# A three-block transformer on one core: the second block's feed-forward network on unnormalised x, its gate product on GpSimd, and the first expert's gather behind its down product

## What is computed

```python
# block 1: 16 experts, each takes the 32 tokens with the largest router weight
gate, idx = lax.top_k(jnp.swapaxes(aff, 1, 2), cap)
xs = jax.vmap(lambda hb, ib: hb[ib])(h, idx)
a, u = einsum(xs, w_gate), einsum(xs, w_up)          # 1024 -> 2048
y = einsum(silu(a) * u, w_down) * gate               # 2048 -> 1024, scattered back and added
...
# block 2
x = x + rmsnorm(merged @ w_out, mix_post_norm)       # norm 6
h = rmsnorm(x, ffn_pre_norm)                         # norm 7
up = causal_dwconv(h @ w_ffn_up, ffn_conv_w, ffn_conv_b)   # 1024 -> 6144, 3 taps along the tokens
f_gate, f_val = jnp.split(up, 2, axis=-1)
f = (gelu(f_gate) * f_val) @ w_ffn_down              # 3072 -> 1024
x = x + rmsnorm(f, ffn_post_norm)                    # norm 8
```

## Time and profile before

| | us |
|---|---|
| median of 3 runs | 1921.76 (1919.69 to 1925.24) |
| the profiled execution | 1920.94 |
| its span, first to last instruction | 1919.2 |
| PE busy in the span | 1516.7 (79%) |
| DVE busy | 717.6 (37%) |
| ACT busy | 597.2 (31%) |
| POOL busy | 36.4 (2%), 40 instructions |

### The profile page before, as it was taken

One profiled execution on the slowest core, in us unless ns is written; L12 is line 12 of the kernel. 1 busy time (PEld: TensorE's weight loads), 2 busy tenths in 40 slices (PEclk: granted clock), 3 DMA queues, 4 the chain that ended last, 5 costly groups with the idle time before them and its releaser, 6 DMA issues.

```text
span 1919.2 us, 25348 instructions
## 1 busy us (share of the span) xinstructions
PE 1516.7 (79%) x10672; PEld 1039.9 (54%) x10672; DVE 717.6 (37%) x1166; ACT 597.2 (31%) x1014; POOL 36.4 (2%) x40
## 2 busy tenths in 40 slices
PE   6999886666665656655666668999999999998897
PEld 4887831111111111111111128999998999898897
DVE  4457600000000000000000006858677886568774
ACT  5434410000000000000000005685666665455653
POOL 0000200000000000000000000000000000000101
PEclk9999897787887887888887779999999999999999
DMA  9556689999999999999999995433363545533330
GB/s 400 220 226 244 264 350 427 429 428 429 428 429 429 429 429 428 429 428 429 429 429 429 428 428 233 182 132 133 140 242 115 193 176 187 189 142 121 137 127 23
DMA packets 48611, 570.30 MB, mean 297 GB/s; under 512 B 4624, under 2 KB 10896, under 8 KB 12048
## 3 DMA queue, kind: packets, MB, share of 16 engines
q1 hardware_dynamic: 43072, 559.96, 71.0%
q10 hardware_dynamic: 5456, 9.15, 1.4%
HBM read 564.89 MB, written 4.19 MB: 297 GB/s over the span
## 4 chain that ended last, share of the span: by engine, by line
PE 50%; DMA 40%; DVE 6%; ACT 3%; issue 1%; POOL 0%; SPq 0%; ACTq 0%; DVEq 0%
PE bank L1521 50%; DMA ring<-in_w_gate 13%; DMA ring<-in_w_up 13%; DMA ring<-in_w_down 12%; ACT work L1922 1%; DMA ring<-in_dense 1%; DVE rstd L2163 1%; ACT weights_high_rounded L1922 1%; DVE ring_rounded L2219 1%; DMA ring<-in_w_ada 1%; ACT L1922 0%; DVE ring_rounded L2230 0%; DVE work L1336 0%; DVE small L1330 0%; DVE small L1316 0%
## 5 line engine op out<-in xcount | busy, mean ns | idle before, releaser
L1521 PE MATMUL bank<-ring,work 128*32 128x512 f32 x3008 | 481.9, 774 | 307.3 <-DMA ring<-in_w_up 126.9
L1521 PEld LDWEIGHTS bank<-ring,work 128*32 128x32 f32 x3008 | 93.2, 126 | 659.3 <-DMA ring<-in_w_up 208.5
L1922 ACT ACTIVATE work<-bank 128x256 f32<-128x256 f32 (+2 forms) x209 | 93.5, 461 | 1089.8 <-PE bank L1521 764.7
L2219 DVE TENSOR_TENSOR ring_rounded<-ring,weights_high_rounded 128x1024 fp32r<-128x1024 f32 x208 | 252.4, 1222 | 118.1 <-ACT weights_high_rounded L1922 117.8
L1922 ACT ACTIVATE weights_high_rounded<-ring 128x1024 fp32r<-128x1024 f32 x244 | 255.3, 1051 | 20.1 <-PE bank L1521 19.7
L2464 DVE TENSOR_TENSOR work<-work,bank 128x512 f32<-128x512 f32 x16 | 16.5, 1033 | 588.8 <-PE bank L1521 588.8
L1521 PE MATMUL bank<-h_high_rounded,weights_high_rounded 128*128 128x256 f32 x1264 | 192.2, 291 | 1.0 <-ACT h_high_rounded L1922 1.0
L1521 PE MATMUL bank<-h_high_rounded,ring_rounded 128*128 128x256 f32 x1264 | 173.1, 278 | 6.3 <-DVE ring_rounded L2219 4.0
L1521 PE MATMUL bank<-h_normed_rounded,weights_high_rounded 128*128 128x256 f32 x1264 | 172.1, 279 | 0.0
L1521 PEld LDWEIGHTS bank<-h_high_rounded,weights_high_rounded 128*128 128x128 f32 x1264 | 165.8, 191 | 11.1 <-issue 10.0
L1521 PEld LDWEIGHTS bank<-h_high_rounded,ring_rounded 128*128 128x128 f32 x1264 | 157.5, 189 | 7.2 <-DVE ring_rounded L2219 4.3
(11 more groups left out here) (248 smaller groups left out, 1265.5 us busy)
## 6 DMA issues: line engine op xcount, KB each, us to landing
ring<-in_w_down SPq DMA_DIRECT2D x64, 2048.0 KB, 16.2
ring<-in_w_gate SPq DMA_DIRECT2D x63, 2048.0 KB, 16.3
ring<-in_w_up SPq DMA_DIRECT2D x61, 2048.0 KB, 16.4
ring<-in_dense SPq DMA_DIRECT2D x60, 2048.0 KB, 7.7
ring<-in_w_ada SPq DMA_DIRECT2D x12, 2048.0 KB, 13.4
work<-in_w_up SPq DMA_DIRECT2D x3, 1024.0 KB, 14.6
bias_diagonals<-work SPq DMA_DIRECT2D x2, 1536.0 KB, 8.8
ring<-in_dense SPq DMA_DIRECT2D x2, 1024.0 KB, 18.5
```

The source lines that it names most:

```text
L1521: return nc.tensor.matmul(o, lhsT, rhs, start=start, stop=stop)
L1922: return nc.scalar.activation(o, i, f, **kw)
L2219: v.tensor_tensor(as_r(w), w, w_high[:, buffer, :], ALU.subtract).then_inc(s.w_low, 1)
```

## The change

- Feed-forward network: PE multiplies x times the norm's gain per channel, not yet divided by the root. `raw_splits` on ACT writes the high halves and squares from X as its tiles come; `add_normed` has a third instruction per tile on DVE, the low half (`split_scaled_low`, already there, an instruction like L2157). PE does the first three units together, tile by tile (`dense_together`); the other units go one by one. The squares of norm 7 are added by POOL, and PE's sum for it stands behind the three units and ahead of the fourth. The matmuls that only kept PE at work are gone there.
- As each unit leaves its bank, DVE multiplies it by the reciprocal root into `SCALED`, four buffers in SBUF (`scaled`). This frees the bank. ACT's tap and DVE's two taps read `SCALED`, a unit later on DVE.
- The gate product and its low half go from DVE to POOL, product k ahead of low half k - 1.
- First expert: `place_slots` goes behind both halves, `gather_rest` behind the down product, and into banks 0 and 1; DVE's copy for expert 1 and ACT's `tokens_in` move accordingly.
- Counts of semaphores in the third block follow.

```diff
@@ -126,7 +126,7 @@
-ADDED_NORMS = (2, 6, 8, 10, 11)
+ADDED_NORMS = (2, 6, 7, 8, 10, 11)
 ADDED_TILES = KT - 2
...
@@ -373,7 +373,7 @@
         UP, FV = tiles3(0, 48), tiles3(48, FT)
-        DO = tiles3(72, 8)
+        DO, SCALED = tiles3(72, 8), tiles3(72, 4)
         LRU_FLAT = tiles(45, 8)
...
@@ -399,6 +399,13 @@
+        def unit_ready(dve, unit):
+            if block_ends(unit):
+                dve.wait_ge(s.ring_used, d2_block(unit) + 1)
+            else:
+                dve.wait_ge(s.dense_mm, units_through(unit))
         def tensor_dense2(pe, dense_unit, unit, act, pu, base=None, first=True, last=True, spare=None):
...
@@ -530,18 +537,13 @@
             awake_through_norm(6, B[6], 4, 4)
-            column_sums(7, spare=B[6])
-            awake_through_norm(7, B[6], 5, 2)
-            for u in range(2 * FT):
-                if u >= 4:
-                    pe.wait_ge(s.conv_step, taps_through(u - 4))
-                unit2(L_UP + u, normed, None if u else "up")
+            dense_together([(d2_block(u), u % UNITS, B[(PU2 + u) % 4], D1_UNITS + u + 1) for u in range(L_UP, L_UP + 3)],
+                           *normed, IN_AT["up"][0])
+            added_sums(7)
+            for u in range(3, 2 * FT):
+                unit2(L_UP + u, normed)
             high, low = by_tile(as_r(UP[:, 0:2 * FT:2, :])), by_tile(as_r(FV))
             for n in range(KT):
-                if n < 4:
-                    pe.wait_ge(s.conv_step, taps_through(2 * FT - 4 + n))
                 for kg in range(3):
...
@@ -696,18 +698,17 @@
             weight_high(D1_UNITS + L_UP - 1 + AHEAD2)
-            squares_of_x(s.x_ready, 2 * KT)
+            raw_splits(2 * KT, HH_plain, par("ffn_pre"))
             root(7)
-            for k in range(KT):
-                split_high(HH[:, k, :], H[:, k, :])
             for u in range(2 * FT):
                 unit_done(d2_block(L_UP + u), block_ends(L_UP + u))
                 if u == 40:
                     act.wait_ge(s.toep_stored, 32)
-                fn(ffn_conved(u), B[(PU2 + L_UP + u) % 4][:, 0:SEQ], ACT.Identity, scale=ffn_weight(u, 2),
-                   bias=par("ffn_conv_b", u, u + 1)).then_inc(s.dense_sb, 1)
+                act.wait_ge(s.dense_sb, PU2 + L_UP + u + 1)
+                fn(ffn_conved(u), SCALED[:, u % 4, :], ACT.Identity, scale=ffn_weight(u, 2),
+                   bias=par("ffn_conv_b", u, u + 1)).then_inc(s.tap_ready, 1)
                 weight_high(D1_UNITS + L_UP + u + AHEAD2)
...
@@ -895,33 +896,37 @@
             dve.wait_ge(s.dense_sb, PU2 + L_UP)
-            add_normed(6, MO2)
+            add_normed(6, MO2, after=lambda k: split_scaled_low(H[:, k, :], X[:, k, :], par("ffn_pre", k, k + 1), HH_plain[:, k, :]))
             weight_low(L_UP - 1 + AHEAD2)
             norm_invert(7)
-            norm_to(7, H, X, par("ffn_pre"), HH)
+            def scaled(u):
+                unit_ready(dve, L_UP + u)
+                v.tensor_tensor(SCALED[:, u % 4, :], B[(PU2 + L_UP + u) % 4][:, 0:SEQ], RS[:, 1, :],
+                                ALU.mult).then_inc(s.dense_sb, 1)
             def tap(u, shift):
                 o = ffn_conved(u)
                 if shift == 1:
-                    dve.wait_ge(s.dense_sb, PU2 + L_UP + u + 1)
+                    dve.wait_ge(s.tap_ready, u + 1)
                 else:
                     dve.wait_ge(s.conv_step, taps_through(u) - 1)
-                v.scalar_tensor_tensor(out=o[:, shift:SEQ], in0=B[(PU2 + L_UP + u) % 4][:, 0:SEQ - shift],
+                v.scalar_tensor_tensor(out=o[:, shift:SEQ], in0=SCALED[:, u % 4, 0:SEQ - shift],
                                        scalar=ffn_weight(u, 2 - shift), in1=o[:, shift:SEQ],
                                        op0=ALU.mult, op1=ALU.add).then_inc(s.conv_step, 1)
-            for k in range(FT):
-                for u in (2 * k, 2 * k + 1):
-                    tap(u, 1)
-                    weight_low(L_UP + u + AHEAD2)
-                    tap(u, 2)
-                    if u % 2 == 0 and k:
-                        split_low(FV[:, k - 1, :], UP[:, 2 * (k - 1), :])
-                dve.wait_ge(s.ffn_gelu, k + 1)
-                dve.wait_ge(s.conv_step, taps_through(2 * k + 1))
-                v.tensor_tensor(FV[:, k, :], FV[:, k, :], UP[:, 2 * k, :], ALU.mult).then_inc(s.act_full, 1)
-            split_low(FV[:, FT - 1, :], UP[:, 2 * (FT - 1), :])
+            for u in range(2 * FT):
+                scaled(u)
+                if u:
+                    tap(u - 1, 1)
+                    weight_low(L_UP + u - 1 + AHEAD2)
+                    tap(u - 1, 2)
+            tap(2 * FT - 1, 1)
+            weight_low(L_DOWN - 1 + AHEAD2)
+            tap(2 * FT - 1, 2)
+            splits_elsewhere(FT)
             weights_low(L_DOWN + AHEAD2, L_EVEN - 1 + AHEAD2)
...
@@ -1009,7 +1014,7 @@
                     if n >= 4:
-                        pe.wait_ge(s.act_full, tile_count("odd_out", n - 4) - KT)
+                        pe.wait_ge(s.act_full, tile_count("odd_out", n - 4) - RAW_SETS * KT)
                     rows = P // len(heads)
...
@@ -1511,7 +1509,22 @@
                 nc.gpsimd.tensor_tensor(as_r(ht), ht, as_r(by_group(HT_HIGH, t, a, b)), ALU.subtract).then_inc(s.ht_low, 1)
-            for i in ADDED_NORMS[1:]:
+            add_squares(6)
+            add_squares(7)
+            def ffn_low(k):
+                pool.wait_ge(s.act_high, tile_count("ffn", k))
+                nc.gpsimd.tensor_tensor(as_r(FV[:, k, :]), FV[:, k, :], as_r(UP[:, 2 * k, :]), ALU.subtract).then_inc(s.act_low, 1)
+            for k in range(FT):
+                pool.wait_ge(s.ffn_gelu, k + 1)
+                pool.wait_ge(s.conv_step, taps_through(2 * k + 1))
+                nc.gpsimd.tensor_tensor(FV[:, k, :], FV[:, k, :], UP[:, 2 * k, :], ALU.mult).then_inc(s.act_full, 1)
+                if k:
+                    ffn_low(k - 1)
+            ffn_low(FT - 1)
+            for i in (8, 10, 11):
                 add_squares(i)
...
@@ -1549,6 +1562,28 @@
                 return ins
+            def dense_together(units, high, low, base):
+                for k in range(KT + 1):
+                    if k < KT:
+                        pe.wait_ge(s.act_high, base + k + 1)
+                        for _, _, bank, counts in units:
+                            if k == 0:
+                                pe.wait_ge(s.w_high, counts)
+                            at = slice(k * P, (k + 1) * P)
+                            mm(bank[:, 0:SEQ], w_high[:, (counts - 1) % HIGHS, at], high[k], k == 0, False)
+                        for block_no, sub, bank, counts in units:
+                            if k == 0:
+                                pe.wait_ge(s.w_low, counts)
+                            mm(bank[:, 0:SEQ], as_r(weights(block_no, sub, k)), high[k], False, False)
+                    if k:
+                        pe.wait_ge(s.act_low, base + k)
+                        for block_no, sub, bank, counts in units:
+                            at = slice((k - 1) * P, k * P)
+                            last = mm(bank[:, 0:SEQ], w_high[:, (counts - 1) % HIGHS, at], low[k - 1], False, k == KT)
+                            if k == KT:
+                                last.then_inc(s.ring_used if sub == UNITS - 1 else s.dense_mm, 1)
...
@@ -1828,11 +1863,10 @@
                         pe.wait_ge(s.xs_sb, k - 1)
-                    gather(k, B[2 + k % 2][:, CAP:], slice(CAP, EXPERTS * CAP))
+                    gather(k, B[k % 2][:, CAP:], slice(CAP, EXPERTS * CAP))
                 pe.wait_ge(s.slots_ready, 1)
                 clear(2)
                 clear(3)
-                pe.wait_ge(s.xs_sb, KT)
...
@@ -1862,8 +1896,8 @@
                             last.then_inc(s.ring_used, 1)
-                    if first:
-                        gather_rest() if half else place_slots()
+                if first:
+                    place_slots()
                 pe.wait_ge(s.hid_ready, e + 1)
...
@@ -1880,6 +1914,8 @@
+                if first:
+                    gather_rest()
                 pe.wait_ge(s.selt_ready, e + 1)
...
@@ -1939,6 +1975,14 @@
                 apart[0] += n
+            def raw_splits(count, high, gain):
+                for k in range(KT):
+                    act.wait_ge(s.x_ready, count + k + 1)
+                    fn(as_r(high[:, k, :]), X[:, k, :], ACT.Identity, scale=gain[:, k:k + 1]).then_inc(s.act_high, 1)
+                    square(k, X[:, k, :])
+                splits_apart(KT)
...
@@ -2093,18 +2137,18 @@
                     act.wait_ge(s.xs_mm, KT + k + 1)
-                    fn(XS[:, k, CAP:EXPERTS * CAP], B[2 + k % 2][:, CAP:], ACT.Identity, scale=ROW_SCALE[:, k:k + 1],
+                    fn(XS[:, k, CAP:EXPERTS * CAP], B[k % 2][:, CAP:], ACT.Identity, scale=ROW_SCALE[:, k:k + 1],
                        bias=ROW_SHIFT[:, k:k + 1]).then_inc(s.xs_sb, 1)
             def expert(e, gates, first=False):
```

(29 more changed lines are left out.)

31 lines of the change are left out of this document (14 added, 17 removed).

## The result

The changed kernel takes 1909.86 us (median of 6 executions, 1901.23 to 1914.63) against 1921.57 of the kernel before beside it; the ratio is 0.9938, 95% interval 0.9922 to 0.9954: faster by 0.6%. Its profiled execution took 1909.62 us, with a span of 1907.8. In a second series (after_again), beside other kernels, the ratio was 0.9942 (0.9927 to 0.9956).

A forecast was written before the change was run, and what follows sets the result against it. Bytes of the experts' weights bound the expert stage, TensorE sets the pace before and behind it. Terms -6.8 - 6.0 + 0.5 = -12.3 us against 1920.94 gave 1908.6, range 1902.0 to 1916.5.

The forecast's parts named there:

- Gather: First expert: slot products moved behind both halves, so SP asks near 257.6 and the 6.8 us DMA pause closes; -6.8 us.
- it just holds: Expert 1 starts near 277.9, frees a slot at 279.9; queued blocks keep DMA busy to 280.8, so no new pause.
- fifth rival: First expert: a pause of the same length opens behind expert 1's fourth block; only the network counts, -5.5, 1915.4; chance 0.06.
- more than 6.8 can't be won: Bound at the first expert: once the 6.8 us pause is closed, bytes are the limit.
- Norm 7: Second block's network: three up units no longer wait for this norm; fifth unit starts at 1467.9 instead of 1473.86, -6.0 us.
- POOL waits until DVE's train has a hole, and DVE isn't slowed: Tile loop of norm 7: POOL does one addition before 1458.7 and the rest behind it, to 1462.7.
- second rival: POOL and DVE hold each other up: norm 7 -7.6, up stage +8.8, gather -6.8; sum -5.6, 1915.3; chance 0.18.
- Up stage: Up units: DVE has four instructions a unit before and after, 2.39 of 2.79 us, PE never waits; 0 us.
- first case: Main forecast: POOL's norm 7 additions are starved behind the tile loop, DVE isn't slowed; 1908.6 us, chance 0.50.
- Down: Start of the down product: the last tile's halves come with cover of 0.3 and 1.2 us; +0.5 us.
- fourth rival: Up stage: the loop of POOL's product takes 6.6 us against 5.58, PE starves; +22, net 1930; chance 0.06.
- The third: Tile loop: DVE's waits leave holes, so POOL's additions meet no hindrance; -6.8 - 10.6 = -17.4, 1903.5; chance 0.20.

The follow-up runs named there:

- after_again: The changed kernel, unaltered, measured once more in a second series beside other kernels; median 1911.31 us, ratio 0.9942 against the kernel before.
- after: The changed kernel itself, with the whole change, against the kernel before; median 1909.86 us, ratio 0.9938.
- product_dve: The changed kernel with the gate product and its low half moved from POOL to DVE, one unit later; 1905.79 us, ratio 0.9934 against the kernel before.
- gather_split: The changed kernel with the gathers of tiles 0 and 1 put between expert 0's third and fourth down blocks; 1907.03 us.
- double_low: The changed kernel with POOL's low half done twice, the first time into a spare tile; 1921.76 us.
- no_adds: The changed kernel without POOL's six additions for norm 7, which is then summed from the first and last tile's squares only; 1908.36 us.
- one_by_tile: The changed kernel with one up unit by tile in the loop instead of three, units 2 to 4 following behind the sum; 1910.33 us.

## Why the prediction was right, and where it was not

**Gather, -6.8 forecast, -4.5 measured.** That the old pause closes, that SP asks at 257.6 and that PE becomes free behind the gather were right: 257.6 is 47.3 us behind norm 5's reciprocal, and so is the 255.89 of after. The failed step is "it just holds". Expert 1 was put at 277.9, 67.6 behind that reciprocal, and came at 280.03, 71.5 behind it: 3.8 us late. First, the fourth down block was put at 261.2 (50.9 behind the mark), from the mean share of a window, 0.23. The mean hides the tail: in the trace of the kernel before that load is issued at 253.93 and lands 9.3 us later, at 263.3 (53.0 behind the mark), and after's lands 52.8 behind it, +1.9. So PE stood 2.27 us where the sum had about 0.4. Second, the lower clock for this block and for the output product, 1.5 + 1.7 us, had no term, although had such a fall. The rest went 1.3 faster than forecast. With the clock kept, that and the late landing nearly cancel, and expert 1 comes at 67.9 (product_dve), as forecast: by luck. What opened is a mild form of the fifth rival.

The bound "more than 6.8 can't be won" also fell: with the clock kept it is 8.1 to 8.4 (1228.11 and 1227.80 against 1236.21). In the middle of the experts' stream the bound nearly holds: there SP's requests come, against the kernel before and counted from norm 5's reciprocal, 3.1 us earlier in after, 6.6 in product_dve and 7.2 in gather_split (medians). About 0.6 more lies behind the experts, between the reciprocals at 1174.41 and 1385.23 of the kernel before: 210.82 us, against 210.1 to 210.2 in all kernels with the moved gather but after_again. The remainder comes late in the experts' stream. Why either comes was not tried.

**Norm 7, -6.0 forecast, -7.6 measured.** The step that failed is "POOL waits until DVE's train has a hole, and DVE isn't slowed". It was read from two old records, in one of which DVE's instruction had started first. double_low shows POOL waiting in just that case; in the tile loop POOL starts first, and DVE waits. The trace shows six additions inside the loop and held DVE instructions; no_adds shows that without them the loop is 2.23 us shorter. This is the second rival's mechanism, whose number for this stage was -7.6; the additions were put behind the three units, to 1462.7, 4.8 us, and cost 2.2 inside the loop. The rest of the chain was sized well: root, reciprocal, scaling, tap and rounding took 1460.11 - 1455.60 = 4.5 us against the 4.6 forecast.

**Up stage, 0 forecast, 0 measured,** for another reason. "Four instructions before, four after" left out that two of them are held, 0.44 and 0.54 us. The second rival had the hold, and its bill of +8.8 was wrong in size: it took 2.39 + 0.60 = 2.99 us a unit, and measured are 2.75, since the busy time of 2.39 held ends that overlap the next start once DVE has no gaps (2.26 back to back), and the hold is 0.49 on average. PE's 2.79 was missed by 0.04. double_low shows how near that was: one instruction more a pair costs 13 us. "L910's mean near 0.48" was the sign of the first case, and it came out 577.

**Down, +0.5 forecast, +1.3 measured.** DVE arrives late from a stage in which it had nothing to spare; PE stands 1.01 us for the last tile's rounding, and none in product_dve.

**Sum.** -4.5 - 7.6 + 1.3 = -10.8; forecast -12.3. With what differed before norm 5 (-1.7) and behind norm 8 (+1.2), where the change alters no work, it is -11.3: 1909.62. Terms wrong by +2.3, -1.6 and +0.8 made a total right to 1.3 us, and the first of them holds a fall of the clock that kernels with the same code there don't always have. That closeness is luck. The chance of 0.50 for the first case was too high: the second rival, with its +8.8 taken out, gives -6.8 - 7.6 + 0.5, that is 1907.0, and has the right mechanism.

**The fourth rival** (the loop of POOL's product) needed POOL instructions of 1.60; they took 0.74 and 0.92. The third needed holes in DVE's train; there were none in which POOL could run for free.

On the shared pair the Trainium skill's page "SBUF — State Buffer" (SBUF: two separate sides) was weighed against the earlier trace rows, and the row was believed. Here it was nearer the truth: its lock takes in instructions of DVE with two SBUF inputs against ones of POOL that read SBUF. Those are what was held (0.91, 0.95, 1.75), while the scaling from a bank was not (0.42 inside POOL's product in one_by_tile). By the page whoever starts first has the pair; the rows of double_low and of the tile loop agree in both directions, and the record at 206.05 still doesn't.
